# A weight set kept over a layer, split ahead of each stage, and column tiles for the samples of the memory attention

## What is computed

```
for i in (0, 1):
    h = rms_norm(x, norm_g[i])
    z = h @ w_in                                  # branch inputs | gate | memory query | memory gate
    branch = pool_mix(...) if i == 0 else stick_breaking(...)
    q = rms_norm(mq, g_q)                         # 4 heads of 128
    p = softmax(q @ mk.T * 128 ** -0.5)           # 256 memory tokens
    mo = p @ mv
    x = x + [branch * silu(gate), mo * silu(mgate)] @ w_out
```

## Time and profile before

| | |
|---|---|
| median of 3 runs | 2871.86 us (2868.12 to 2877.64) |
| the profiled execution | 2869.99 us, span 2868.3 us |
| mean granted clock of PE | 0.921 |
| busy in the span | PE 2497.8 us (87%), PEld 72%, DVE 39%, ACT 28%, POOL 6% |
| stages, start in us | front 7, pooling 129, memory 496, out 749, norm 976, projection 1013, memory 1620, stick-breaking 1876, out 2642 |

### The profile page before, as it was taken

How to read it: one execution, slowest core, us unless ns; L and a number is a source line. 1 busy time by engine, 2 the same in 40 slices (tenths; PEclk the granted TensorE clock), 3 DMA queues, 4 the chain that set the end, 5 groups by cost and what they waited for, 6 DMA issues and landing times. The chain is left out here.

```text
span 2868.3 us, 42799 instructions
## 1 busy us (share of the span) xinstructions
PE 2497.8 (87%) x17317; PEld 2069.5 (72%) x17317; DVE 1110.8 (39%) x1842; ACT 797.3 (28%) x1514; POOL 161.2 (6%) x331
## 2 busy tenths in 40 slices
PE   5599998996599779999999798747999999996899
PEld 4599997986578679999999797634555554542787
DVE  5323133114221320111111102248888888875311
ACT  4321110222210221112110012124555555555200
POOL 0000000100000000000001110011111111100000
PEclk8799999988699789999999897768999999998899
DMA  5412201120533322243231102177999999974532
GB/s 174 137 54 77 76 33 39 45 88 3 207 114 96 99 95 98 98 135 120 90 112 46 68 15 88 45 243 249 340 357 350 345 362 336 369 273 148 169 88 68
DMA packets 202814, 426.35 MB, mean 149 GB/s; under 512 B 22965, under 2 KB 115233, under 8 KB 202601
## 3 DMA queue, kind: packets, MB, share of 16 engines
q1 hardware_dynamic: 192025, 386.53, 38.9%
q0 software_dynamic: 10592, 37.10, 3.5%
HBM read 361.75 MB, written 62.37 MB: 148 GB/s over the span
## 5 line engine op out<-in xcount | busy, mean ns | idle before, releaser
L80 PE MATMUL i_bank<-h_hT_hi,i_w_hi 128*128 128x352 f32 x864 | 281.0, 325 | 15.7 <-DVE i_w_lo L1295 15.7
L80 PE MATMUL o_bank<-o_w_hi,o_y_hi 128*128 128x512 f32 x576 | 229.6, 399 | 58.5 <-DVE o_w_lo L1159 58.0
L82 PE MATMUL i_bank<-h_hT_hi,i_w_lo 128*128 128x352 f32 x864 | 278.3, 322 | 0.0
L81 PE MATMUL i_bank<-h_hT_lo,i_w_hi 128*128 128x352 f32 x864 | 278.2, 322 | 0.0
L1778 DVE STREAM_TRANSPOSE b_kt<-b_kraw 128x768 f32<-128x768 f32 x256 | 248.2, 970 | 16.1 <-DMA b_kraw<-in_cache_sb_k_dram 16.1
L81 PE MATMUL o_bank<-o_w_lo,o_y_hi 128*128 128x512 f32 x576 | 228.0, 396 | 0.0
L82 PE MATMUL o_bank<-o_w_hi,o_y_lo 128*128 128x512 f32 x576 | 227.8, 395 | 0.0
L80 PE MATMUL p_bank<-h_hT_hi,p_w_hi 128*128 128x352 f32 x576 | 187.0, 325 | 11.5 <-DVE p_w_lo L655 11.5
L81 PE MATMUL p_bank<-h_hT_lo,p_w_hi 128*128 128x352 f32 x576 | 185.5, 322 | 0.0
L82 PE MATMUL p_bank<-h_hT_hi,p_w_lo 128*128 128x352 f32 x576 | 185.2, 322 | 0.0
L80 PEld LDWEIGHTS i_bank<-h_hT_hi,i_w_hi 128*128 128x128 f32 x864 | 163.2, 189 | 16.1 <-DVE i_w_lo L1295 16.1
(11 more groups left out here) (262 smaller groups left out, 4817.4 us busy)
## 6 DMA issues: line engine op xcount, KB each, us to landing
b_kraw<-in_cache_sb_k_dram SPq DMA_DIRECT2D x256, 384.0 KB, 5.4
b_vpage<-in_cache_sb_v_dram SPq DMA_DIRECT2D x128, 768.0 KB, 6.3
i_w<-in_w_in_sb_dram SPq DMA_DIRECT2D x16, 1536.0 KB
o_y<-scratch_yT SPq DMA_DIRECT2D x18, 1024.0 KB, 6.6
o_w<-in_w_out_dram SPq DMA_DIRECT2D x16, 1024.0 KB
p_w<-in_w_in_pool_dram SPq DMA_DIRECT2D x8, 1536.0 KB
f_w<-in_w_mem_kv_dram SPq DMA_DIRECT2D x8, 1024.0 KB
a_mk<-in_cache_mem_k_dram SPq DMA_DIRECT2D x16, 512.0 KB, 3.6
```

The source lines that it names most:

```text
L80: pe.matmul(out, stat_hi, mov_hi, start=first, stop=False)
L81: pe.matmul(out, stat_hi, mov_lo, start=False, stop=False)
L82: return pe.matmul(out, stat_lo, mov_hi, start=False, stop=last)
```

## The change

One set `w`, `w_hi`, `w_lo` of 384 columns now lives as long as the layer's `hT`, with three semaphores. It takes the place of each phase's buffers of index 0. Ahead of its end a phase fetches the next phase's chunk 0 into it (`load_ahead` on SP), rounds it (`high_ahead` on ACT) and subtracts (`low_ahead` on DVE): front for pooling, pooling for the memory products, norm for the second projection, and that one for the memory products. A phase then starts with chunk 1's load, and PE waits for `ahead_lo` in place of the first `w_lo`. The memory products have two buffers `w` in place of one.

In the memory attention, `mk` becomes three buffers in the layer's `w`, the first three keys and the prompt's own keys and values are loaded during the products, key transposes alternate between banks 4, 5 and 0, 1, and `mkT` holds four samples. `qpad` has 32 columns per sample and head; the four samples of a group stand in four column tiles of 32 (partitions 32 l to 32 l + 31 of the bank). The sample values take the probabilities as the 32 stationary columns and 512 value columns as the moving side, inside the tile loop after the scores of tiles 4 and 6; ACT copies each group's result into `vev`, and at the end `sample_select` picks each head's part with the identity into the transposed layout, for one gating. POOL does two of the four normalizations.

```diff
+def load_ahead(sp, c, n, src):
+
+    cols = src.shape[1]
+    sp.dma_start(c["w"][:, :, 0:cols], src.rearrange("(k p) n -> p k n", p=P)).then_inc(c["ahead_loaded"], 16)
+
+
+def high_ahead(act, c, n, cols):
+
+    act.wait_ge(c["ahead_loaded"], 16 * (n + 1))
+    act.activation(c["w_hi"][:, :, 0:cols], c["w"][:, :, 0:cols], ACT.Copy).then_inc(c["ahead_hi"], 1)
+
+
+def low_ahead(dve, c, n, cols):
+
+    dve.wait_ge(c["ahead_hi"], n + 1)
+    dve.tensor_tensor(c["w_lo"][:, :, 0:cols], c["w"][:, :, 0:cols], c["w_hi"][:, :, 0:cols].bitcast(F32),
+                      ALU.subtract).then_inc(c["ahead_lo"], 1)
+
...
                 for t in range(N):
+                    if t == 2:
+                        load_ahead(sp, c, 0, A["w_in_sb"][0][:, 0:KU])
...
                         evacuate(t - 1)
+                    if t == 3:
+                        high_ahead(act, c, 0, KU)
...
                         rest(t - 1)
+                    if t == 3:
+                        low_ahead(dve, c, 0, KU)
...
+        w = [c["w"][:, :, 0:WC], k.sb("w1", [P, KD, WC])]
+        w_hi = [c["w_hi"][:, :, 0:WC], k.sb("w_hi1", [P, KD, WC], F32R)]
+        w_lo = [c["w_lo"][:, :, 0:WC], k.sb("w_lo1", [P, KD, WC], F32R)]
...
+                 8: [("K", 1), ("P", 6), ("W", 7), ("X", 0), ("P", 7), ("V", 1)]}
...
+                sp.wait_ge(s["wlo"], 7)
+                load_ahead(sp, c, 0, A["w_in_pool"][0][:, 0:KU])
...
+                        if what == "X":
+                            act.wait_ge(s["made"], 14)
+                            high_ahead(act, c, 0, KU)
...
+                sp.dma_start(w[1][:, :, :], w_src[:, offset(1):offset(1) + KU].rearrange("(k p) n -> p k n", p=P)
+                             ).then_inc(wl[1], 16)
...
-                        sp.wait_ge(s["wlo"], j - 1)
+                load_group(0)
+                for j in range(2, 2 * GROUPS):
+                    if j >= 3:
+                        sp.wait_ge(s["wlo"], j - 2)
...
+                sp.wait_ge(s["wlo"], 2 * GROUPS - 2)
+                load_ahead(sp, c, 1, w_src[:, 2 * BW:2 * BW + 2 * P])
                 finish_group(sp, GROUPS - 1)
...
                         part(2 * g + 2)
+                    else:
+                        act.wait_ge(s["uready"], 9 * (2 * GROUPS - 1))
+                        high_ahead(act, c, 1, 2 * P)
...
+                    else:
+                        low_ahead(dve, c, 1, 2 * P)
...
+                        pe.wait_ge(s["wlo"] if g + half else c["ahead_lo"], 2 * g + half if g + half else 1)
...
-        sq = k.sb("sq", [P, MH, T])
+        sqm = k.sb("sq", [P, MH * T])
-        qpad = k.sb("qpad", [P, NB_S * MH * (R + T_S)])
+        BL, BG = 4, NB_S // 4
+        CT = BG * MH * T_S
+        qpad = k.sb("qpad", [P, NB_S, MH, CT])
+        mk = c["w"][:, :, :].rearrange("p k n -> p (k n)").rearrange("p (b j n) -> p b j n", b=3, j=MJ)
...
+                for j in range(1, 4):
+                    if j == 3:
+                        sp.wait_ge(s["wlo"], 1)
+                    sp.dma_start(w[j % 2][:, :, :], w_src[:, off:off + WC].rearrange("(k p) n -> p k n", p=P)
+                                 ).then_inc(wl[j % 2], 16)
+                sp.dma_start(c["mkT"][:, :, :].rearrange("p h m -> p (h m)"), S["mkT"][i]).then_inc(s["own"], 16)
+                sp.dma_start(c["mv"][:, :, :], O["mem_v"][i, 0].rearrange("(j p) h d -> p j (h d)", p=P)
+                             ).then_inc(s["own"], 16)
+                sp.wait_ge(s["wlo"], 2)
+                for b in range(3):
+                    load_memory_keys(sp, b)
...
+                    for g in range(BG):
+                        gp.tensor_copy(qv[:, g, :, h, g, h, :], qT[:, h, SEQ + g * BL * T_S:SEQ + (g + 1) * BL * T_S].rearrange(
+                            "p (l t) -> p l t", t=T_S)).then_inc(s["padded"], 1)
...
+                    pe.wait_ge(s["wlo"] if j else c["ahead_lo"], j if j else 2)
...
+        mv = sqm[:, 0:BL * MJ * MW].rearrange("p (b j n) -> p b j n", b=BL, j=MJ)
+        vev = k.sb("vev", [P, BG, MW])
...
+                    if b >= 3:
+                        sp.wait_ge(s["ktr"], 2 * (b - 2))
+                        load_memory_keys(sp, b)
+                sp.wait_ge(s["mean"], 1)
+                    if b >= BL:
+                        sp.wait_ge(s["spv"], b // BL)
+                    sp.dma_start(mv[:, b % BL, :, :], A["cache_mem_v"][i, b].rearrange("(j p) h d -> p j (h d)", p=P)
+                                 ).then_inc(vl[b % BL], 16)
...
+                    if t == 2:
+                        act.wait_ge(s["str_"], 1)
+                        act.activation(psT[:, :, :], bank[7][:, MEM:2 * MEM].rearrange("p (j r) -> p j r", j=MJ),
+                                       ACT.Copy).then_inc(s["spt"], 1)
+                    if t in (4, 6):
+                        g = (t - 4) // 2
+                        act.wait_ge(s["spv"], g + 1)
+                        act.activation(vev[:, g, :], bank[7][:, :], ACT.Copy).then_inc(s["sve"], 1)
...
-                    for h in range(MH):
+                    for h in range(2):
...
+                dve.wait_ge(s["sel"], 1)
+                dve.tensor_tensor(gate[:, :, SEQ:T], bank[7][:, 0:R].rearrange("p (h c) -> p h c", h=MH), gate[:, :, SEQ:T],
+                                  ALU.mult).then_inc(s["sym"], 1)
+            @block.gpsimd
+            def _(gp):
+                for t in range(TILES):
+                    gp.wait_ge(s["rec"], t + 1)
+                    for h in range(2, MH):
+                        gp.tensor_scalar(e[:, t % 2, h, :], e[:, t % 2, h, :], rsum[:, t % 2, h:h + 1], None, ALU.mult
+                                         ).then_inc(s["nrmP"], 1)
...
+                    pe.wait_ge(kl[b % 3], 16 * (b // 3 + 1))
+                    if b >= 2:
+                        pe.wait_ge(s["kev"], b - 1)
+                        pe.wait_ge(s["kevD"], b - 1)
...
+                                ins = pe.transpose(bank[(4, 0)[b % 2] + q][:, hh * MEM + j * P:hh * MEM + (j + 1) * P],
...
+                        for l in range(BL):
+                            ins = pe.matmul(bank[7][l * CT:(l + 1) * CT, 0:MEM], qpad[:, g * BL + l, h, :], mkT[:, l, h, :],
+                                            start=g == 0 and h == 0, stop=g == BG - 1 and h == MH - 1)
...
+                for g in range(BG):
+                    for l in range(BL):
+                        turn_keys(g * BL + l)
+                    sample_scores(g)
...
+                def sample_values(g):
+                    pe.wait_ge(s["spt"], 1)
+                    if g:
+                        pe.wait_ge(s["sve"], g)
+                    for l in range(BL):
+                        pe.wait_ge(vl[l], 16 * (g + 1))
+                    for j in range(MJ):
+                        for l in range(BL):
+                            ins = pe.matmul(bank[7][l * CT:(l + 1) * CT, :], psT[:, j, l * CT:(l + 1) * CT], mv[:, l, j, :],
+                                            start=j == 0, stop=j == MJ - 1)
+                    ins.then_inc(s["spv"], 1)
+
+                def sample_select():
+                    pe.wait_ge(s["sve"], BG)
+                    pick = c["ident"][:, :].rearrange("p (l g h t) -> p g h l t", l=BL, g=BG, h=MH)
+                    place = bank[7][:, 0:R].rearrange("p (h g l t) -> p g h l t", h=MH, g=BG, l=BL)
+                    for g in range(BG):
+                        for h in range(MH):
+                            ins = pe.matmul(place[:, g, h, :, :], vev[:, g, h * HD:(h + 1) * HD], pick[:, g, h, :, :],
+                                            start=True, stop=True)
+                    ins.then_inc(s["sel"], 1)
...
                         scores(t + 1)
+                    if t == 1:
+                        sample_turned()
+                    if t in (3, 5):
+                        sample_values((t - 3) // 2)
                     pe.wait_ge(s["nrm"], t + 1)
+                    pe.wait_ge(s["nrmP"], 2 * (t + 1))
...
+                sample_select()
...
+                sp.wait_ge(s["wlo"], 14)
+                load_ahead(sp, c, 1, w_src[:, 4 * BW:4 * BW + 2 * P])
...
+                act.wait_ge(s["vready"], 3 * N)
+                high_ahead(act, c, 1, 2 * P)
...
+                    if u == 3 * N + 2:
+                        low_ahead(dve, c, 1, 2 * P)
...
+                        pe.wait_ge(s["wlo"] if j else c["ahead_lo"], j if j else 1)
...
+                c["w"] = kh.sb("w", [P, KD, KU])
+                c["w_hi"], c["w_lo"] = (kh.sb(n, [P, KD, KU], F32R) for n in ("w_hi", "w_lo"))
+                c["ahead_loaded"], c["ahead_hi"], c["ahead_lo"] = (
+                    kh.sem(n) for n in ("ahead_loaded", "ahead_hi", "ahead_lo"))
```

More of the change, by code:

```diff
@@ L481, in _ @@
                     for what, n in after.get(t, ()):
-                        if what not in "PV":
+                        if what == "X":
+                            low_ahead(dve, c, 0, KU)
```

(14 more changed lines are left out.)

164 lines of the change are left out of this document (53 added, 111 removed), and 1 row of the table after.

## The result

The changed kernel took 2794.05 us, the median of four runs (2789.06 to 2799.44); the kernel before took 2871.9 us beside it (2868.12 to 2877.64). The ratio is 0.973, with a 95% interval of 0.971 to 0.975. The forecast was 2779, the range 2761 to 2802. The gain is 77.8 us by the medians where 90.6 were worked out.

A forecast was written before the change was run, and what follows sets the result against it. PE, busy 87% of the span, was taken as the bound; gains were sought where it waits or does little. Terms 7.5 + 9.5 + 9.3 + 6.5 + 10.4 + 52.4 - 4 - 1 = 90.6 us gave 2779 us, range 2761 to 2802.

The forecast's parts named there:

- Part 1: Start of the pooling stage: chunk 0 split under cover in the front stage, PE starting at about 140; gain 7.5 us.
- Part 2: Two starts of the memory products: PE begins when the stage does; gains 9.5 and 9.3 us.
- rival (b): PE keeps its high clock across closed gaps, at memory starts and selections: 8 us more gain, 2771 us; chance 0.06.
- Part 3: Start of the second projection: 13.6 us gained, norm stage 7 us longer for the split; net 6.5 us.
- rival (c): Stages begin no earlier because something else is last; half of the seams' 33 us goes: 2796 us; chance 0.08.
- The microsecond for the barriers: Clearing the layer's own semaphores and meeting at a barrier twice: 1 us lost, bounds 0 and 3.
- Part 4: Key loop of the memory attention: column tiles cut PE's work, then loads bind; gain 5.2 us a layer, 10.4 in all.
- rival (a): Column tiles do not overlap with four on one PSUM bank, so the key loop gains near nothing: 2805 us; chance 0.06.
- Part 5: Samples' values, moved from the memory attention's end into its tile loop: gain 52.4 us, bounds 48 and 56.
- Part 6: Tile loop of the memory attention, two of four normalizations on POOL: 4 us lost, bounds -5 and +14.
- The worst case that was worked out: Tile loop: DVE's 0.57 and POOL's 1.0 us add up to 1.6, a loss of 0.45 us per tile.
- Rival (d): POOL's two heads take over the tile loop; at 4 us a head the kernel is slower, 2885 us; chance 0.02.

The follow-up runs named there:

- the halves: The changed kernel with each of POOL's two heads normalized in two instructions of 128 columns instead of one of 256: 2809.9 us, ratio 0.979.

## Why the prediction was right, and where not

The direction and the range were right. Of the terms, the tile loop was badly mis-sized, and the key loop, the norm stage and the samples' values erred the other way, by 1, 1 and 3 us.

**Part 1** said 7.5 us, PE at about 140: it began on the state at 140.08, the first product follows at 140.60, against 147.58: 7.0. The copy fitted where it was said to, 118.85 for 119.2.

**Part 2** said 9.5 and 9.3: 9.6 and 9.3. Of rival (b), PE keeping its clock, almost nothing came: after 4.25 us of idle time the first product took 0.40 us at a granted clock of 1.00, the second 0.43 as it fell, the third 0.50 at half clock. At the second memory start, after 6.9 us, the first product already took 0.63 us at half clock.

**Part 3** said 6.5 net, with the norm stage 7 longer: it is 6.0 to 6.1 longer and the net gain 7.6. Tile 2 was 1.8 us late instead of 3. Moving this seam alone was not tried; the kernel with all seams late had a norm stage of 37.9 us. Parts 1 to 3 together: 32.8 forecast, 32.9 by experiment, 30.9 by its stages. The four executions of the changed kernel alone spread over 10 us, so this is no proof to the microsecond, but it leaves no room for rival (c) and its 16 us. The microsecond for the barriers is not seen.

**Part 4** said 10.4: the key loop took 20.2 and 18.5 us against 24.3 and 25.7, 11.3 in all. The tiles' instructions are 0.06 us apart, as taken, in three groups of four (0.11 in the one at half clock), so rival (a) falls.

**Part 5** said 52.4: behind the loop 2.4 us are left of 30.8, and in the second layer 2.6 of 30.0, 55.8 us. The selection took 2.1 and 2.3 us and not 3.7. The row that it was priced from ran at a granted clock of 0.50; the selections had 0.88 and 0.79, which is the other half of rival (b), and it came true: 3 us.

**Part 6** is the term that was mis-sized: 4 us lost were forecast, bounds -5 to +14, and 26.6 were lost. Two things in it. First, "its two-input product takes 1.95 us for 1056 columns, which makes 0.4 to 0.6 us for a head of 256": a head takes 0.92 to 0.99. I divided a long instruction by its columns and gave a short one of another form the same rate and no fixed part; the halves show 0.28 us fixed and 2.5 ns a column. Even the product's own form has a fixed part: from 1.14 us for 512 columns and 1.95 for 1056 I estimate 0.38 us and 1.5 ns a column, 0.76 us for 256. From DVE's first normalization to PE's transposes it is now 2.1 us (666.74 to 668.88), where it was 1.2 and 1.6 was the worst that I took: 0.94 us a tile, 15 us in all. Second, the clock. I had put a half-clock price on the ends of gaps (rival (b)) and none on a wait that grows inside a loop: 3.2 us instead of 2.3 ahead of the transposes. Value products at half clock (3.3 to 3.8 us and not 2.0) were 11 of 16 before and are 15 of 16 now. The first layer's row before, against 28.5 us now:

```profile
L1069 PE MATMUL a_bank<-a_pT,mem_mv 128*128 128x128 f32 x128 | 23.6, 361 | 6.7 <-ACT a_pT L876 5.0 <-DVE a_pT L990 0.9 <-issue 0.8
```

PE's own account of both loops says how much each is. Its waits ahead of the transposes grew from 37.0 to 44.3 us and the samples' values, which lie in four of them, add 7.7: together the 15. Value products took 56.0 us instead of 49.1, the scores 33.8 instead of 31.4, the transposes 21.7 instead of 19.4, with as many instructions: 11.6 us for the clock. Together 26.6. Filling the wait gave 26.

The rule of the Trainium skill ("SBUF — State Buffer", on which operations grab the shared pair) would have made the term 8 us. What it describes is seen in the runs with one long POOL instruction, but as the cause of this loss it is small: DVE's 0.2 us a tile end at 667.57, hidden behind POOL's end at 668.78, and POOL's own slowing is 0.15 us, 2.4 of the 15 us. The worst case that was worked out, both in series at 0.45 us a tile, stood on the assumed rate; the bound of 14 us allowed for twice that, and was too low all the same. Rival (d) had the right mechanism, POOL in each tile's path, with 4 us a head where 1 was measured. The sign at which I said the prediction would be wrong, tiles over 10 us, did show (668.88 to 679.25 is 10.4), and it cost the forecast its middle but not its range. That is luck in part: part 5 gave 3 us more than said, and the median run is 5 us under the profiled one, which at 2799.4 is near the upper end of 2802. The two output projections are 1.2 us longer each; 1.8 us of the 2.4 are PE's waits for `o_w_lo`, 59.8 against 58.0 in all, and why these grew is open.

The sum again, against the traces: 7.0 + 18.9 + 7.6 + 11.3 + 55.8 - 26.6 - 3.1 (output projections and stick-breaking) = 70.9, where 70.6 were measured.

**A version that beats both.** The change with all heads on DVE and the normalization ahead of the next maxima takes 2742 us, 52 less than the changed kernel and 130 less than the one before.

## What to carry to other kernels

A price from a long instruction is not one for a short one: look for a row of the same form and about the same columns, and if there is none, put the fixed part (here 0.28 us of 0.92) and a slower form into the bad bound. Work handed to an idle engine is free only if something runs beside it. Here PE already waited for that very step, and putting the step earlier in DVE's order was worth more than sharing it out. Where PE waits in every round of a loop, price one microsecond more of waiting together with what it may do to the clock of the matmuls behind it.
